# The second mixer's second gate as four seven-product pairs, with the forms made beside the first gate

## The chip, the core and the metric

The kernel runs on one core of one Trainium2 chip. The metric is device time in microseconds (us) for one execution, the median of several; the profile is of one execution.

## The reference

Two transformer blocks are applied to 512 tokens of 1024 features in float32: a first mixer, an MLP with a gated side input, a second mixer and a second MLP. The change lies in the second mixer. There a normed input is projected, two branches are computed (`ya`, a windowed attention, and `yb`, a gated linear attention), each goes through a matrix of its own, and two gates weigh them:

```
h = rmsnorm(x, ln_mix_g[l]);  z = h @ w_in[l];  qa, ..., ga, gb = split_cols(z)
merged = sigmoid(ga) * (ya @ w_branch_a[l]) + sigmoid(gb) * (yb @ w_branch_b[l])
x = x + merged @ w_out[l]
```

Every matrix here has 1024 columns, that is 8 output tiles of 128; `h`, `yb` and `merged` are 1024 wide (8 input blocks of 128), `ya` is 512 wide (4 blocks).

## The kernel before

Activations lie feature by feature: 128 partitions x 8 blocks x 512 tokens. A *tile* is one output of 128 features x 512 tokens in a bank of PSUM. It is summed over its blocks, and each block takes three matmuls of 512 columns (L1728 to L1730), because both operands are split in a high and a low part (`AH`/`AL` for the normed input, `WH`/`WL` for weights): high x high, low x high, high x low.

Weights stream in *chunks* of eight blocks (512 KB). SyncE loads a chunk into one of three raw buffers (`w_load`, L1645), ScalarE copies it to the high part (`w_hi`, L2156), VectorE makes the low part (`w_lo`, L2561). Four converted units are held (`NW`); a conversion waits until the unit four before it has been used. `ahead` says the conversion of three units ahead when TensorE begins a chunk, and `rest` says the low part and the load from the fifth block on.

A *pair* (`pair`) computes two output tiles of one normed input by seven products instead of eight, over halves of the tokens (256 columns) and halves of the input blocks. Each product is 12 matmuls of 256 columns (L1709 to L1711). The order of products is

```
SLOTS = (1, 5, 6, 2, 7, 3, 4)
```

and a pair needs four converted units from its two chunks: sums of weights (`s_add` 1 and 2, kept in `WS`), the first chunk (with high and low part whole), half a chunk (`s_add` 4, whose copy is L2154) and the second chunk (after `s_add` 3). `s_snap` has ScalarE copy a finished product from PSUM (`SN`) so that the bank can go on summing: product 6 waits for the snapshot of product 1, product 4 for that of product 7. VectorE then adds what is missing (`s_c11`, `s_c12`, `s_c22`). The input side of products 5, 6, 7 and 4 are four *forms* of the normed input: `t_diff` (GpSimd, L3363), `t_u` (ScalarE), `t_2`, `t_3`, `t_4` (VectorE), and then `t_split` 1 to 4, in which ScalarE makes the high part (L2182 for form 1 in four pieces, L2186) and VectorE the low part (L2635, L2640). Form 4 is written over a part of `AH`/`AL`, so it waits for the last plain tile. Before the change pairs serve the first MLP (stage "2") and the second (stage "5"); each stage has buffers of its own, a fourth raw buffer (`WX`) among them.

One order is written out by hand, step by step (`say`), and each engine's program takes its steps from it in that order; an engine waits for semaphores where a step needs another engine's. `beside` runs a list of steps alongside the blocks (one `tick` per block, two per product of a pair), `finish` says what is left of them at once, `align` fills the running chunk with empty blocks.

At the end of the second mixer (`mixer2`) the order of TensorE is: first gate tiles 0 and 1, then tile m of branch a and gate tile m+2 in turn, two tiles of the second gate, then tile m of branch b and second-gate tile m+2 in turn (all plain tiles of eight blocks, those of branch a of four), and the output projection (`mix2`). For a gate tile VectorE multiplies by the norm's factor (`scaled`, L2971) and ScalarE takes the sigmoid (L2482, L2487). Branch b is multiplied by its gate (L3222), added to branch a's (L3226), and split for the output projection (L2491, L2655). Six empty blocks stand ahead of the second MLP's first down blocks, where `align` is called; the gates begin two blocks into a chunk.

Of the kernel before, what the change touches and what calls it, by code (L numbers as in the profile page):

```python
# [196 lines left out]
class Order:  # L197


    def __init__(self, sections=()):  # L200
        self.found = []
        self.cut = set()
        self.npairs = 0
        self.pair_of = {}
        self.last_plain = {}
        self.in_stage = {}
        self.last_pair = {}
        self.units = []
# [184 lines left out]
    def forms(self, s, n=5):  # L393

        self.say("t_diff", s)
        yield 4
        self.say("t_u", s)
        yield 3
        self.say("t_2", s)
        yield 3  # L400
        self.say("t_3", s)
        yield 3
        self.say("t_4", s)
        yield 3
        for j in range(1, n):
            self.say("t_split", s, j)
            yield 3
# [604 lines left out]
    def mixer2(self, post):  # L1012
# [57 lines left out]
        def gate_a(m):  # L1070
            t = self.tile(fm(at("ga", 128 * m)), A)
            self.say("gate_a", m, t)
            self.close(t)
        gate_a(0)
# [273 lines left out]
class Memory:  # L1348
    def __init__(self, nc, dram, psum):
# [96 lines left out]
        self.MGL = at("MGL", 90, [128, 8, T], F32R)  # L1446
        self.GA = at("GA", 78, [128, 2, T])
        self.GB = at("GB", 66, [128, 4, T])
# [14 lines left out]
        self.AC4 = at("AC4", 110.25, [128, T])  # L1463
# [31 lines left out]
    def x(self, kind, j):  # L1495

        h, l = {"A": (self.AH, self.AL), "B1": (self.BH, self.BL), "D1": (self.DH, self.DL), "C1": (self.CHh, self.CLl),
                "F1": (self.FH1, self.FL1), "P1": (self.PH, self.PL), "Y2": (self.YAH, self.YAL),
                "Z2": (self.YBH, self.YBL), "M2": (self.MGH, self.MGL), "F2": (self.FH2, self.FL2)}[
                    "A" if kind[0] == "A" else kind]  # L1500
        if kind in ("F1", "F2"):
            j = j % (FS if kind == "F1" else FS2)
        return h[:, j, :], l[:, j, :]

    def raw(self, b):

        return self.WR[:, b, :] if b < NRAW else (self.WX1, self.WX2)[b - NRAW][:]

    def t_raw(self, s, j):

        if j < 4:
            return (self.TW1 if s == "2" else self.TW2)[:, j - 1, :, :]
        return self.sn(s)[:, :, :]

    def t_form(self, s, j):

        if j < 4:
            h, l = (self.TH1, self.TL1) if s == "2" else (self.TH2, self.TL2)
            return h[:, j - 1, :, :], l[:, j - 1, :, :]
        return tuple(a[:, :, :].rearrange("p (i q) t -> p i q t", q=2)[:, :, 0, T // 2:] for a in (self.AH, self.AL))  # L1520
# [9 lines left out]
    def sn(self, s):  # L1530
        return self.SN1 if s == "2" else self.SN2
# [6 lines left out]
    def ws(self, s):  # L1538
        return self.WS1 if s == "2" else self.WS2
# [77 lines left out]
def sync_program(e, w, order, at, m):  # L1617
# [17 lines left out]
    def w_load(c):  # L1635
# [7 lines left out]
        elif b >= NRAW:  # L1643
            w.wait_ge(*at("rbc", "25"[b - NRAW]))
# [28 lines left out]
def tensor_program(e, w, order, at, m):  # L1673
# [262 lines left out]
    def values1(u, t):  # L1936
# [12 lines left out]
        ins.then_inc(*at.up("values1", "values1", u))  # L1949
# [86 lines left out]
    def values2(u, t):  # L2036
# [12 lines left out]
        ins.then_inc(*at.up("values2", "values2", u))  # L2049
# [93 lines left out]
def scalar_program(e, w, order, at, m):  # L2143
# [25 lines left out]
    def t_u(s):  # L2169
        w.wait_ge(*at("rbc", s))  # L2170
        for i in range(4):
# [5 lines left out]
    def t_split(s, j):  # L2177
        h, x = m.t_form(s, j)[0], m.t_raw(s, j)
        w.wait_ge(*at(("t_diff", "t_2", "t_3", "t_4")[j - 1], s))
        if j == 1:  # L2180
# [56 lines left out]
    def exp1(u):  # L2237
# [3 lines left out]
        if u >= 2:  # L2241
            w.wait_ge(*at("turn1", u - 2))
        e.activation(m.PB1[:, u % 2, 0:W], m.SB1[:, u % 2, 0:W], ACT.Exp, scale=-1.0, bias=col[:, 0:1],
                     accum_out=col[:, 1:2]).then_inc(*at.up("exp1", "exp1", u))

    def scale1(u):
        p = m.PB1[:, u % 2, 0:128 * (unit1(u)[1] + 1)]
        w.wait_ge(*at("recip1", u))
        e.activation(p, p, ACT.Copy, scale=m.ST1[:, 6 + 3 * u:7 + 3 * u]).then_inc(*at.up("probs1", "probs1", u))

    def turned1(u, t):
# [5 lines left out]
        e.activation(m.PT1[:, u % 2, 0:W], m.bank[t.bank][:, 0:W], ACT.Copy).then_inc(*at.up("turned1", "turned1", u))  # L2257
# [124 lines left out]
    def exp2(u):  # L2382
# [3 lines left out]
        for g in range(2):  # L2386
            s = m.SB2[:, u % 2, W * g:W * g + W]
            e.activation(s, s, ACT.Exp, scale=-1.0, bias=col(g), accum_out=col(6 + g)).then_inc(*at.up("exp2", "exp2", u, g))
        w.wait_ge(*at("sink2", u))
        e.activation(col(4, 2), col(2, 2), ACT.Exp).then_inc(*at.up("exp2", "exp2", u))  # L2390

    def scale2(u):
        W = 256 if u % 4 else 128
        w.wait_ge(*at("recip2", u))
        for g in range(2):
            s = m.SB2[:, u % 2, W * g:W * g + W]
            e.activation(s, s, ACT.Copy, scale=m.WST[:, 10 * u + 8 + g:10 * u + 9 + g]).then_inc(
                *at.up("probs2", "probs2", u))

    def turn2(u, t):  # L2400
# [5 lines left out]
        e.activation(m.PT2[:, u % 2, 0:W], m.bank[t.bank][:, 0:W], ACT.Copy).then_inc(*at.up("turned2", "turned2", u))  # L2406
# [77 lines left out]
    def gate_b(i, t):  # L2484
        g = m.GB[:, i % 4, :]
        w.wait_ge(*at("gate_b", i))
        e.activation(g, g, ACT.Sigmoid).then_inc(*at.up("gate_sig", "gb_sig", i))  # L2487

    def branch_b(i, t):
# [35 lines left out]
    def ffn_u(f, t):  # L2525
        if f < 6:
# [10 lines left out]
           "gn_out": gn_out, "vb": vb, "rb_silu": rb_silu, "ya_split": ya_split, "gate_a": gate_a, "gate_b": gate_b,  # L2537
           "branch_b": branch_b, "ffn_a": ffn_a, "ffn_u": ffn_u}
# [5 lines left out]
def vector_program(e, w, order, at, m):  # L2544
# [18 lines left out]
    def s_add(c, j):  # L2563
# [4 lines left out]
        if j == 1:  # L2568
            w.wait_ge(*at("w_raw", c + 1))
            w.wait_ge(*at("rbc", s))  # L2570
            if order.units_before(c) is not None:
                w.wait_ge(*at("w_lo", order.units_before(c)))
# [32 lines left out]
    def t_2(s):  # L2605
        w.wait_ge(*at("t_diff", s))
# [154 lines left out]
    def scale1(u):  # L2761
        col = m.ST1[:, 4 + 3 * u:7 + 3 * u]
        w.wait_ge(*at("exp1", u))
        e.reciprocal(col[:, 2:3], col[:, 1:2]).then_inc(*at.up("recip1", "recip1", u))
# [304 lines left out]
    def scale2(u):  # L3069
        col = lambda i, k=1: m.WST[:, 10 * u + i:10 * u + i + k]  # L3070
        w.wait_ge(*at("exp2", u))
        for g in range(2):
            e.tensor_scalar(col(6 + g), col(6 + g), col(4 + g), None, ALU.add).then_inc(*at.up("recip2", "total2", u))
        w.wait_ge(*at("total2", u))
        e.reciprocal(col(8, 2), col(6, 2)).then_inc(*at.up("recip2", "recip2", u))
# [134 lines left out]
    def gate_b(i, t):  # L3210
        if i >= 4:
            w.wait_ge(*at("x_lo", "M2", i - 4))
        else:
            w.wait_ge(*at("yb", 7))
        scaled(m.GB[:, i % 4, :], t, "4").then_inc(*at.up("gate_b", "gate_b", i))
        at.also(("gate_b", i), "read", t.id)

    def branch_b(i, t):
# [8 lines left out]
        low("M2", i, g)  # L3227
# [84 lines left out]
    def y_base(i):  # L3312
# [17 lines left out]
           "gate_a": gate_a, "branch_a": branch_a, "gate_b": gate_b, "branch_b": branch_b, "mix2": mix2, "ffn_a": ffn_a,  # L3330
# [6 lines left out]
def gpsimd_program(e, w, order, at, m):  # L3337
# [19 lines left out]
    def t_diff(s):  # L3357
        for i in range(0, 8, 2):
            for b in range(2):
                w.wait_ge(*at("h", s, i, b))  # L3360
        x = m.H[:, :, :].rearrange("p (i q) t -> p i q t", q=2)[:, :, 0, :]
# [309 lines left out]
```

## Time and profile before

| what | value |
|---|---|
| three runs | 1427.6, 1427.9, 1428.74 us; median 1427.9 |
| the profiled execution's own time | 1427.68 us |
| its span, first to last instruction | 1425.9 us |
| busy | PE 1413.9, DVE 986.4, ACT 647.0, POOL 214.8 us |
| granted TensorE clock, mean | 0.998 |

PE is TensorE's matmuls, PEld its weight loads, DVE VectorE, ACT ScalarE, POOL GpSimd, SP SyncE. Starts are us from the span's start. A matmul's end in the trace is modelled, and the next starts before it; the spacing of starts tells what one costs.

### The profile page before, as it was taken

The page shows a single profiled execution, that of the slowest core. Times are in us where ns is not written, and L with a number is a line of the kernel's source. Part 1 is how long each engine was busy: PE and PEld are TensorE (multiplying, and loading weights), DVE is VectorE, ACT ScalarE, POOL GpSimd, SP SyncE. Part 2 cuts the span into 40 slices and gives each one's busy share as a digit, 9 for nine tenths or more (in the row PEclk, how much of TensorE's full clock was granted, in tenths as well). Part 3 has the DMA queues.
Part 4 walks back from the last instruction along what each step waited for, and adds up shares of the span by engine and source line. Part 5 has one row for each costly group of instructions (what it writes and reads, how often), then busy time and mean ns, then how long its engine had stood idle before and what let it go on. Part 6 is the DMA issues. An engine that isn't in the chain of part 4 may idle for free.

```text
span 1425.9 us, 20562 instructions
## 1 busy us (share of the span) xinstructions
PE 1413.9 (99%) x8054; PEld 1213.9 (85%) x8054; DVE 986.4 (69%) x1537; ACT 647.0 (45%) x1028; POOL 214.8 (15%) x136
## 2 busy tenths in 40 slices
PE   9999999999999999999999999999999999999998
PEld 6776798889989888887799888888888889999997
DVE  5777477876676657897696736534452888888877
ACT  5345535534345434545464546323332545455450
POOL 4175224000000011330052104000021000000000
PEclk9999999999999999999999999999999999999999
DMA  6222212333233332222211211323323233333331
GB/s 242 89 75 69 65 60 89 100 97 115 93 100 104 119 104 74 89 67 82 74 60 41 65 45 59 110 90 101 98 90 92 87 105 103 103 93 116 104 106 73
DMA packets 36352, 130.00 MB, mean 91 GB/s; under 512 B 4040, under 2 KB 4296, under 8 KB 36256
## 3 DMA queue, kind: packets, MB, share of 16 engines
q1 hardware_dynamic: 35968, 128.44, 28.5%
q8 instruction: 64, 1.05, 0.3%
q14 instruction: 32, 0.26, 0.1%
q10 hardware_dynamic: 288, 0.26, 0.1%
HBM read 126.56 MB, written 2.10 MB: 90 GB/s over the span
## 4 chain that ended last, share of the span: by engine, by line
PE 91%; DVE 5%; ACT 2%; issue 1%; DMA 1%; ACTq 0%; DVEq 0%; SPq 0%
PE P L1728 17%; PE P L1730 16%; PE P L1729 16%; PE P L1709 5%; PE P L1711 5%; PE P L1710 5%; PE P L1776 4%; PE P L1767 4%; PE P L1769 4%; PE P L2069 2%; DVE WL L2561 1%; PE P L1816 1%; PE P L1817 1%; PE P L1818 1%; PE P L1924 1%
## 5 line engine op out<-in xcount | busy, mean ns | idle before, releaser
L2156 ACT ACTIVATE WH<-WR 128x1024 fp32r<-128x1024 f32 x212 | 223.6, 1055 | 259.2 <-PE P L1730 181.4
L2561 DVE TENSOR_TENSOR WL<-WR,WH 128x1024 fp32r<-128x1024 f32 x196 | 265.5, 1355 | 103.0 <-ACT WH L2156 102.6
L1728 PE MATMUL P<-AH,WH 128*128 128x512 f32 x456 | 186.2, 408 | 0.2 <-DVE BC L3002 0.2
L1730 PE MATMUL P<-AH,WL 128*128 128x512 f32 x456 | 178.2, 391 | 0.0
L1729 PE MATMUL P<-AL,WH 128*128 128x512 f32 x456 | 177.8, 390 | 0.0
L1728 PE MATMUL P<-FH,WH 128*128 128x512 f32 x432 | 168.5, 390 | 0.5 <-issue 0.3
L1729 PE MATMUL P<-FL,WH 128*128 128x512 f32 x432 | 168.4, 390 | 0.0
L1730 PE MATMUL P<-FH,WL 128*128 128x512 f32 x432 | 168.1, 389 | 0.0
L3375 POOL TENSOR_TENSOR AC<-AC,SQ 128x512 f32<-128x512 f32 x27 | 42.5, 1573 | 506.7 <-ACT SQ L2211 505.8
L1709 PE MATMUL P<-AH,WH 128*128 128x256 f32 x400 | 113.5, 284 | 0.3 <-ACT SN L2167 0.2
L1711 PE MATMUL P<-AH,WL 128*128 128x256 f32 x400 | 113.2, 283 | 0.0
L1710 PE MATMUL P<-AL,WH 128*128 128x256 f32 x400 | 113.2, 283 | 0.0
L1728 PEld LDWEIGHTS P<-AH,WH 128*128 128x128 f32 x456 | 85.7, 188 | 21.1 <-issue 4.5
L1730 PEld LDWEIGHTS P<-AH,WL 128*128 128x128 f32 x456 | 85.6, 188 | 18.6
L1729 PEld LDWEIGHTS P<-AL,WH 128*128 128x128 f32 x456 | 85.9, 188 | 16.3 <-issue 0.5
L1767 PE MATMUL P<-AH,WH 128*128 128x512 f32 (+1 forms) x264 | 96.0, 371 | 1.9 <-ACT AH L2202 1.6
L1728 PEld LDWEIGHTS P<-FH,WH 128*128 128x128 f32 x432 | 81.2, 188 | 17.5 <-issue 0.7
L1769 PE MATMUL P<-AH,WL 128*128 128x512 f32 (+1 forms) x264 | 95.2, 367 | 0.8 <-DVE WL L2561 0.5
L1730 PEld LDWEIGHTS P<-FH,WL 128*128 128x128 f32 x432 | 81.1, 188 | 17.1
L1729 PEld LDWEIGHTS P<-FL,WH 128*128 128x128 f32 x432 | 81.2, 188 | 15.8
L1709 PE MATMUL P<-TH,WH 128*128 128x256 f32 x300 | 84.9, 283 | 0.0
L1710 PE MATMUL P<-TL,WH 128*128 128x256 f32 x300 | 84.9, 283 | 0.0
(409 smaller groups left out, 3148.0 us busy)
## 6 DMA issues: line engine op xcount, KB each, us to landing
WR<-in_ws SPq DMA_DIRECT2D x212, 512.0 KB, 3.5
WX<-in_ws SPq DMA_DIRECT2D x21, 512.0 KB, 3.5
out<-Y SPq DMA_DIRECT2D x8, 256.0 KB, 2.0
H<-in_xT SPq DMA_DIRECT2D x3, 512.0 KB, 8.0
C<-in_const SPq DMA_DIRECT2D x1, 946.5 KB, 11.0
H<-in_xT SPq DMA_DIRECT2D x2, 256.0 KB, 4.4
PR<-in_pT SPq DMA_DIRECT2D x1, 512.0 KB, 4.9
WR<-in_ws SPq DMA_DIRECT2D x1, 384.0 KB, 4.8
```

Of the source, the lines that this page charges most:

```text
L1709: e.matmul(P, wh, xh, start=k in (1, 5, 2) and i == 0, stop=False, skip_group_check=True)
L1710: e.matmul(P, wh, xl, start=False, stop=False, skip_group_check=True)
L1711: ins = e.matmul(P, wl, xh, start=False, stop=k in (2, 3, 4) and i == 3, skip_group_check=True)
L1728: e.matmul(P, wh, xh, start=start, stop=False)
L1729: e.matmul(P, wh, xl, start=False, stop=False)
L1730: ins = e.matmul(P, wl, xh, start=False, stop=stop)
L1767: e.matmul(P, m.WH[:, c % NW, o:o + 128], xh, start=start, stop=False, skip_group_check=True)
L1769: e.matmul(P, m.WL[:, c % NW, o:o + 128], xh, start=False, stop=False, skip_group_check=True)
L1776: ins = e.matmul(m.bank[t.bank][:, cols(a)], wh, m.x(*x)[1][:, cols(a)], start=False, stop=stop, skip_group_check=True)
L2156: e.activation(H, w_source(m, order, k), ACT.Copy).then_inc(*at.up("w_hi", "w_hi", k))
L2561: e.tensor_tensor(L, w_source(m, order, k), H, ALU.subtract).then_inc(*at.up("w_lo", "w_lo", k))
L3375: e.tensor_tensor(AC, AC, m.square(n, i)[:, cols(a)], ALU.add).then_inc(*at.up("summed", "summed", n, i, parts(a)[0]))
```

## The change

The second gate's eight tiles become four pairs (stage "4"), each followed by two tiles of branch b. The forms are made beside the first gate: the raw ones from the fifth tile of branch a on, the splits after the last tile of the first gate. `align` is called ahead of the first pair, and six banks serve the ring during the pairs. The split of a merged tile becomes a step of its own (`merged_split`), said one block after an even tile, and inside the next pair after an odd one. Stage "4" gets buffers of its own (a fourth raw buffer `WX3`, loaded once `yb` is done), others move to make room, and some semaphores of steps that never run together are merged. The total number of blocks stays 1872. Steps for a first gate in pairs (`kind` "a", `gated_a`, `branch_a_copy`) are written but not called.

```diff
-        for s, buffer in (("2", NRAW), ("5", NRAW + 1)):
+        for s, buffer in (("2", NRAW), ("5", NRAW + 1), ("4", NRAW + 2)):
...
             t = self.tile(specs, [("Y2", j) for j in range(4)])
-            self.finish((lambda: self.yb == 8) if m < 4 else (lambda: self.gated))
+            if m < 5:
+                self.finish((lambda: self.yb == 8) if m < 4 else None)
+            if m == 4:
+                self.beside(self.raws("4", 3))
             self.say("branch_a", m, t)
             self.close(t)
             if m < 6:
-                gate_a(m + 2)
-
-        def gate(m):
-            t = self.tile(fm(at("gb", 128 * m)), A)
-            self.say("gate_b", m, t)
-            self.close(t)
-        gate(0)
-        gate(1)
+                t = gate_a(m + 2)
+            if m == 5:
+                self.last_plain["4"] = t
+                self.beside(self.splits("4", range(1, 5), 3))
         self.finish()
-        for m in range(8):
+        self.banks = (0, 1, 2, 3, 6, 7)
+        self.align()
+
+        def post(p):
+            kind, i = p.f
+            self.say("gate_first", p, kind, i)
+            self.say("gate_sig", kind, i)
+            yield 1
+            self.say("gate_second", p, kind, i + 1)
+            self.close(p.x)
+            self.say("gate_sig", kind, i + 1)
+            yield 2
...
+        def pair(kind, i):
+            c0 = at("g" + kind, 128 * i)
+            self.pair("4", fm(c0), fm(c0 + 128), (kind, i), post)
+
+        def branch(m):
             t = self.tile([block("w_branch_b_2", 128 * q, 128 * m) for q in range(8)], [("Z2", q) for q in range(8)])
             self.say("branch_b", m, t)
             self.close(t)
-            if m < 6:
-                gate(m + 2)
+            self.beside(merged(m))
+
+        def merged(m):
+            yield 10 if m % 2 and m < 7 else 1
+            self.say("merged_split", m)
+        for m in range(0, 8, 2):
+            pair("b", m)
+            branch(m)
+            branch(m + 1)
+        self.finish()
+        self.banks = (0, 1, 2, 3)
...
+    def gate_first(p, kind, i):
+        gate_free(kind, i)
+        w.wait_ge(*at("s_c11", p.id))
+        w.wait_ge(*at("s_c12", p.id))
+        e.tensor_tensor(m.gate(kind, i), m.snap(p, 0, 2), m.RBC3[:], ALU.mult).then_inc(
+            *at.up("gate_" + kind, "gate_" + kind, i))
+
+    def gate_second(p, kind, i):
+        g = m.gate(kind, i)
+        gate_free(kind, i)
+        w.wait_ge(*at("s_full", p.id, 4))
+        e.tensor_tensor(g[:, cols(0)], m.bank[p.x.bank][:, cols(0)], m.RBC3[:, cols(0)], ALU.mult).then_inc(
+            *at.up("gate_" + kind, "gate_half", kind, i))
+        at.also(("gate_half", kind, i), "read", p.x.id)
+        w.wait_ge(*at("s_c22", p.id))
+        e.tensor_tensor(g[:, cols(1)], m.snap(p, 3), m.RBC3[:, cols(1)], ALU.mult).then_inc(
+            *at.up("gate_" + kind, "gate_" + kind, i))
+        at.also(("gate_" + kind, i), "sn_free", p.id)
...
+    def merged_split(i):
+        low("M2", i, m.GB[:, i % 4, :])
```

## Rows read from the trace of the kernel before

**Rows 1.** The page: busy time, share, instructions by engine; the chain that ended last.

```profile
PE 1413.9 (99%) x8054; PEld 1213.9 (85%) x8054; DVE 986.4 (69%) x1537; ACT 647.0 (45%) x1028; POOL 214.8 (15%) x136
...
PE 91%; DVE 5%; ACT 2%; issue 1%; DMA 1%; ACTq 0%; DVEq 0%; SPq 0%
```

**Rows 2.** Timeline of TensorE, second gate and branch b: start, duration, line, operation.

```profile
939.81 0.39 PE L1728 MATMUL P<-AH,WH 128*128 128x512 f32 x1
...
1026.85 0.39 PE L1728 MATMUL P<-MGH,WH 128*128 128x512 f32 x1
```

**Rows 3.** Timeline of TensorE, a pair of the first MLP.

```profile
299.37 0.28 PE L1709 MATMUL P<-AH,WH 128*128 128x256 f32 x1
...
309.44 0.40 PE L1728 MATMUL P<-FH,WH 128*128 128x512 f32 x1
```

**Rows 4.** Windows: a pair's period in the first MLP; the gate stage.

```profile
core 0: us, PE busy (x) PEld busy (x) DVE busy (x) ACT busy (x) POOL busy (x), PEclk, DMA share, GB/s
...
299.37:320.35 20.98, 20.98 (x134) 19.09 (x133) 14.52 (x20) 8.88 (x13) 0.00 (x0) 1.00 0.32 101
...
945.00:1031.00 86.00, 86.00 (x381) 71.20 (x380) 40.30 (x48) 26.25 (x32) 0.00 (x0) 1.00 0.30 92
```

**Rows 5.** Timeline of TensorE and VectorE, last MLP, around its first pairs.

```profile
1158.83 0.39 PE L1728 MATMUL P<-FH,WH 128*128 128x512 f32 x1
...
1163.45 1.22 DVE L2561 TENSOR_TENSOR WL<-WR,WH 128x1024 fp32r<-128x1024 f32 x1
...
1164.77 0.47 PE L1728 MATMUL P<-FH,WH 128*128 128x512 f32 x1 [0.33 <-issue]
...
1170.31 0.28 PE L1709 MATMUL P<-AH,WH 128*128 128x256 f32 x1
...
1180.71 0.40 PE L1728 MATMUL P<-FH,WH 128*128 128x512 f32 x1
...
1210.96 0.39 PE L1709 MATMUL P<-AH,WH 128*128 128x256 f32 x1 [0.19 <-ACT SN L2167]
```

**Rows 6.** Tiles of forms and snapshots: duration ns min/median/max, first and last start.

```profile
L2167 ACT ACTIVATE SN<-P x100: 360/384/388, 280.5 to 1381.0; 128x256 f32<-128x256 f32 x100
...
L2182 ACT ACTIVATE TH<-TW,PM x8: 493/495/498, 266.1 to 1145.0; 128x256 fp32r<-128x256 f32 x8
L2635 DVE SCALAR_TENSOR_TENSOR TL<-TW,PM,TH x8: 477/480/485, 267.9 to 1146.8; 128x256 fp32r<-128x256 f32 x8
L2186 ACT ACTIVATE TH<-TW x4: 1042/1044/1045, 267.7 to 1147.3; 128x1024 fp32r<-128x1024 f32 x4
L2640 DVE TENSOR_TENSOR TL<-TW,TH x4: 1219/1221/1226, 269.5 to 1149.4; 128x1024 fp32r<-128x1024 f32 x4
L3363 POOL TENSOR_TENSOR TW<-H x2: 2404/2786/3167, 229.0 to 1076.0; 128x1024 f32<-128x1024 f32 x2
```

**Rows 7.** Timeline of ScalarE and VectorE at the last tile of the first gate.

```profile
934.64 0.69 DVE L2971 TENSOR_TENSOR GA<-P,RBC 128x512 f32<-128x512 f32 x1 [3.69 <-PE P L1730]
...
935.25 1.22 DVE L2561 TENSOR_TENSOR WL<-WR,WH 128x1024 fp32r<-128x1024 f32 x1
...
935.37 0.63 ACT L2482 ACTIVATE GA<-GA 128x512 f32<-128x512 f32 x1 [1.03 <-DVE GA L2971]
```

**Rows 8.** Timeline of VectorE and TensorE at the first pair of the first MLP.

```profile
276.94 1.22 DVE L2561 TENSOR_TENSOR WL<-WX,WH 128x1024 fp32r<-128x1024 f32 x1
...
277.88 0.39 PE L1730 MATMUL P<-FH,WL 128*128 128x512 f32 x1
278.31 0.36 PE L1709 MATMUL P<-AH,WH 128*128 128x256 f32 x1
```

**Rows 9.** Timeline of VectorE and ScalarE, last MLP: fourth weight sum, half copy.

```profile
1182.87 0.69 DVE L2581 TENSOR_TENSOR WR<-WR,WS 128x512 f32<-128x512 f32 x1
...
1183.59 0.63 ACT L2154 ACTIVATE WH<-WR 128x512 fp32r<-128x512 f32 x1 [3.33 <-DVE WR L2581]
```

More of the change, by code:

```diff
@@ L393, in forms, with raws, splits @@
     def forms(self, s, n=5):
+        yield from self.raws(s, 3)
+        yield from self.splits(s, range(1, n), 3)
+    def raws(self, s, pace):
         self.say("t_diff", s)
-        yield 4
+        yield pace + 1
         self.say("t_u", s)
-        yield 3
+        yield pace
         self.say("t_2", s)
-        yield 3
+        yield pace
         self.say("t_3", s)
-        yield 3
+        yield pace
         self.say("t_4", s)
-        yield 3
-        for j in range(1, n):
+        yield pace
+    def splits(self, s, js, pace):
+        for j in js:
             self.say("t_split", s, j)
-            yield 3
+            yield pace
     def narrow(self, name, c0, n, kind):
@@ L1073, in gate_a @@
             self.close(t)
+            return t
         gate_a(0)
@@ L1498, in x @@
                 "F1": (self.FH1, self.FL1), "P1": (self.PH, self.PL), "Y2": (self.YAH, self.YAL),
-                "Z2": (self.YBH, self.YBL), "M2": (self.MGH, self.MGL), "F2": (self.FH2, self.FL2)}[
+                "Z2": (self.YBH, self.YBL), "M2": (self.MGH, (self.MGLA, self.MGLB)[j // 4 % 2]), "F2": (self.FH2, self.FL2)}[
                     "A" if kind[0] == "A" else kind]
+        if kind == "M2":
+            return h[:, j, :], l[:, j % 4, :]
         if kind in ("F1", "F2"):
@@ L1505, in raw @@
     def raw(self, b):
-        return self.WR[:, b, :] if b < NRAW else (self.WX1, self.WX2)[b - NRAW][:]
+        return self.WR[:, b, :] if b < NRAW else (self.WX1, self.WX2, self.WX3)[b - NRAW][:]
     def t_raw(self, s, j):
         if j < 4:
+            if s == "4":
+                return self.TW3A[:, 0, :, :] if j == 1 else self.TW3B[:, j - 2, :, :]
             return (self.TW1 if s == "2" else self.TW2)[:, j - 1, :, :]
@@ L1517, in t_form @@
         if j < 4:
+            if s == "4":
+                l = self.TL3A[:, 0, :, :] if j == 1 else self.TL3B[:, j - 2, :, :]
+                return self.TH3[:, j - 1, :, :], l
             h, l = (self.TH1, self.TL1) if s == "2" else (self.TH2, self.TL2)
@@ L1530, in sn, with gate @@
     def sn(self, s):
-        return self.SN1 if s == "2" else self.SN2
+        return {"2": self.SN1, "4": self.SN3, "5": self.SN2}[s]
+    def gate(self, kind, i):
+        return self.GA[:, i % 2, :] if kind == "a" else self.GB[:, i % 4, :]
     def snap(self, p, j, n=1):
@@ L1538, in ws @@
     def ws(self, s):
-        return self.WS1 if s == "2" else self.WS2
+        return {"2": self.WS1, "4": self.WS3, "5": self.WS2}[s]
     def sq(self, n):
@@ L2179, in t_split @@
         w.wait_ge(*at(("t_diff", "t_2", "t_3", "t_4")[j - 1], s))
+        if s == "4" and j < 4:
+            w.wait_ge(*at("x_lo", "Z2", 2 * j - 1))
         if j == 1:
@@ L2256, in turned1 @@
             w.wait_ge(*at("values1", u - 2))
-        e.activation(m.PT1[:, u % 2, 0:W], m.bank[t.bank][:, 0:W], ACT.Copy).then_inc(*at.up("turned1", "turned1", u))
+        e.activation(m.PT1[:, u % 2, 0:W], m.bank[t.bank][:, 0:W], ACT.Copy).then_inc(*at.up("turned", "turned1", u))
         at.also(("turned1", u), "read", t.id)
@@ L2405, in turn2 @@
             w.wait_ge(*at("values2", u - 2))
-        e.activation(m.PT2[:, u % 2, 0:W], m.bank[t.bank][:, 0:W], ACT.Copy).then_inc(*at.up("turned2", "turned2", u))
+        e.activation(m.PT2[:, u % 2, 0:W], m.bank[t.bank][:, 0:W], ACT.Copy).then_inc(*at.up("turned", "turned2", u))
         at.also(("turned2", u), "read", t.id)
@@ L2482, in gate_a, with gate_sig, branch_a_copy @@
         e.activation(g, g, ACT.Sigmoid).then_inc(*at.up("gate_sig", "ga_sig", i))
[L2484 to L2489, printed above, removed]
+    def gate_sig(kind, i):
+        g = m.gate(kind, i)
+        w.wait_ge(*at("gate_" + kind, i))
+        e.activation(g, g, ACT.Sigmoid).then_inc(*at.up("gate_sig", "g%s_sig" % kind, i))
+    def branch_a_copy(i, t):
+        w.wait_ge(*at("full", t.id))
+        w.wait_ge(*at("yb", 7))
+        if i >= 4:
+            w.wait_ge(*at("gn_gated", 7))
+        e.activation(m.MG[:, i, :], m.bank[t.bank][:], ACT.Copy).then_inc(
+            *at.up("branch_a_copy", "branch_a_copy", i))
+        at.also(("branch_a_copy", i), "read", t.id)
+    def merged_split(i):
         w.wait_ge(*at("merged", i))
@@ L3208, in branch_a, with gated_a, gate_free @@
         at.also(("branch_a", i), "read", t.id)
-    def gate_b(i, t):
-        if i >= 4:
-            w.wait_ge(*at("x_lo", "M2", i - 4))
-        else:
-            w.wait_ge(*at("yb", 7))
-        scaled(m.GB[:, i % 4, :], t, "4").then_inc(*at.up("gate_b", "gate_b", i))
-        at.also(("gate_b", i), "read", t.id)
+    def gated_a(i):
+        x = m.MG[:, i, :]
+        w.wait_ge(*at("branch_a_copy", i))
+        w.wait_ge(*at("ga_sig", i))
+        e.tensor_tensor(x, x, m.GA[:, i % 2, :], ALU.mult).then_inc(*at.up("branch_a", "branch_a", i))
+    def gate_free(kind, i):
+        if kind == "a":
+            w.wait_ge(*at("branch_a", i - 2))
+        else:
+            w.wait_ge(*(at("x_lo", "M2", i - 4) if i >= 4 else at("gn_gated", 7)))
+    def gate_first(p, kind, i):
[5 more added lines that the diff above has]
+    def gate_second(p, kind, i):
+        g = m.gate(kind, i)
+        gate_free(kind, i)
[7 more added lines that the diff above has]
+        at.also(("gate_" + kind, i), "sn_free", p.id)
     def branch_b(i, t):
@@ L3226, in branch_b, with merged_split @@
         e.tensor_tensor(g, g, m.MG[:, i, :], ALU.add).then_inc(*at.up("branch_b", "merged", i))
-        low("M2", i, g)
+    def merged_split(i):
+        low("M2", i, m.GB[:, i % 4, :])
     def mix2(i, t):
```

55 lines of the change are left out of this document (38 added, 17 removed).

## The prediction, made before the result was known

> **What bounds the kernel now.** I read the page first. TensorE is busy for 99% of the span and fills 91% of the chain that ended last [rows 1]. So a part of this change counts only if it makes TensorE's queue shorter or makes TensorE wait. Next I read the timeline of TensorE over the stage. The first matmul of the second gate starts at 939.81 and the first of the output projection at 1026.85 [rows 2]. Between them lie 16 plain tiles of 24 matmuls: 87.04 us, 5.44 us a tile, 0.2267 us a matmul of 512 columns, without a hole. Third, the timeline of the first MLP, which has pairs already: a pair starts at 299.37 and the plain blocks behind it at 309.44 [rows 3]; the next pair follows 20.98 us after the first [rows 4]. So the 84 matmuls of a pair take 10.07 us (0.12 us each), where the two plain tiles that they replace take 10.88. Fourth, the windows: over one such period of 20.98 us VectorE is busy for 14.52 and ScalarE for 8.88, in the present gate stage for 40.30 and 26.25 of 86 [rows 4]. Neither is the bound on average, so the rest is a matter of order.
>
> **The change, part by part.** *Removed:* eight plain gate tiles, 8 x 5.44 = 43.52 us of TensorE, with eight VectorE multiplies of 512 columns. *Added on TensorE:* four pairs, 4 x 10.07 = 40.28. The eight tiles of the second branch stay. In steady state the stage costs four periods of pair and 16 blocks, which is the period in rows 4: 4 x 20.98 = 83.92 against 87.04, **-3.1 us**. That is 7%, not the 12.5% of saved columns, because a matmul of half the columns costs 0.53 of a full one.
>
> The Trainium skill, "TensorE: Matmul & The Clock Gate", section "Back-to-back issue gap", gives 262 cycles for 256 columns and 518 for 512; an estimate by these would be 9.2 against 10.4 us, so about 4.8 us for four pairs. The row has 10.07 against 10.88, and the sum goes by the row.
>
> *Added on the other engines per pair:* four sums of weights (0.69 each), four weight splits (three of 1.22 us on VectorE, one of 0.69) in place of two of 1.22, four snapshots on ScalarE (0.38 each [rows 6]), three half-width combinations, and the two gates. From the 14.52 us of VectorE in rows 4 I take off the first MLP's own work in that period (two relu squares, two splits, three accumulations: 4.8 us) and add the gates (0.69 + 2 x 0.42), and multiply, add and split for two branch tiles (6 x 0.69): 15.4 of 20.98. That hides behind the pair. Without this cover each added VectorE microsecond would cost one. The weight transfers are the same in number, and a fourth raw buffer is added for this stage; the first MLP has the same four chunks a period and no hole, so I cost them at nothing.
>
> *The forms:* one GpSimd subtraction (2.4 to 3.2 us [rows 6]); on ScalarE four small scalings and then the splits (four of 0.495 and three of 1.04, 5.1 us); on VectorE twelve small operations and the low parts (four of 0.48 and three of 1.22). The first half, up to the raw forms, is queued behind the fifth tile of branch a, some 19 us before the first pair. VectorE has idle stretches there, so it costs nothing. The splits are queued only behind the last gate tile, and that is eight blocks (5.44 us) before the pair. Here I follow the queues of both engines, since each takes its steps in the written order. The times are those of the timeline of before, in which the pair's first product would be due at 939.81.
>
> - VectorE multiplies the last gate tile at 934.64, the sigmoid follows at 935.37 and ends at 936.0 [rows 7]. Only then comes form 1 on ScalarE: four pieces, 1.7 us as a row of four, to 937.6. VectorE, which used to split weights at 935.25 [rows 7], is now queued behind form 1 and idles until 937.7; its four pieces end at 939.3.
> - Behind them stands the low part of the pair's first weight chunk: 1.22 us, to 940.5. TensorE needs it for the first product. In the first MLP such a split began at 276.94 and the pair at 278.31 [rows 8], so 0.15 us pass from its end to TensorE. The pair starts at 940.65, **0.84 us late**.
> - Behind that split VectorE makes the fourth weight sum (0.69, to 941.3). ScalarE's half copy must wait for it, as in the last MLP, where the sum starts at 1182.87 and the copy at 1183.59 [rows 9]. Forms 3 and 4 are queued behind this copy, then the full copy of the second chunk, and only then the snapshot of the first product. That is 0.63 + 2 x 1.04 + 1.06 + 0.38, less about 0.1 of overlap at each step: the snapshot ends near 945.1. The third product adds into the same bank and waits for it. It was due two products (2 x 1.44) after the start, at 943.6, so **1.65 us more**.
> - VectorE meanwhile has form 2, two branch products, forms 3 and 4 and two weight splits, near 947.6. The fifth product needs the last of these at 948.1: just hidden.
>
> The first pair therefore costs **+2.5 us**. From below this is bounded by nothing at all (if the queues drained as in the first MLP, whose first pair began 0.43 us after the matmul before it, 0.2 late [rows 8]); from above by about 3.2, if these operations run 10% slower side by side and the fifth product waits too. I take the worked chain.
>
> *Moved:* the alignment. The gate's pairs must start on a chunk, so six empty blocks are put in here, and the six that stood ahead of the last MLP's first down blocks go. There TensorE now loses time: a chunk takes from 1158.83 to 1164.77, 0.50 more than 5.44 and 0.07 behind it, and a weight split of VectorE ends just before, at 1163.45 + 1.22; the pair after it takes 10.40 instead of 10.07 [rows 5]. With a whole chunk ahead, that split comes 4 us earlier. I take the 0.57 back, **-0.6**; the bounds are 0 and -0.9. The buffer moves and the merged semaphores add no instruction, and the output projection keeps its order: its last operand is split while its first seven blocks run, as before.
>
> **The sum.** -3.1 + 2.5 - 0.6 = -1.2 us, against the profiled execution's own 1427.68 (span 1425.9, 1.78 around it): 1426.5. The median of the three runs lies 0.2 above that execution, so I predict 1426.7. A difference under 0.2%, 2.9 us, can't be told from no change here.
>
> **The rivals.**
> - *The cover suffices.* The splits drain as in the first MLP and the first pair loses 0.3 instead of 2.5: 1424.5 with the 0.2 of the median. For it: every steady pair there runs without a hole [rows 3]. Against: there the forms had 32 more blocks of cover; here they have eight. Chance 0.15.
> - *Half the columns, half the time.* If 256 columns took half of 0.2267, a pair would take 9.52, 5.4 us saved in four: 1424.4. The Trainium skill's page named above leans that way. Against: the row of 10.07. Chance 0.03.
> - *Every later pair waits too: slower.* The split of the merged odd tile stands on ScalarE ahead of the snapshot of the fifth product, which the seventh and last waits for. A pair of the last MLP already waits there (1210.96 [rows 5]). The fifth product ends 7.2 us into its pair; with that split (0.63) and its own 0.38 the snapshot ends near 7.95, and the last product is due at 8.64, 0.7 later. If it comes more than 0.7 us late, three pairs pay the excess; at 2.1 us late each pays 1.4 and the time is 1430.9. Against: VectorE is less loaded here than in the last MLP, and the period is that of the first. Chance 0.06.
> - *More comes back in the last MLP, or the stall is smaller by a microsecond.* 1425.4. Chance 0.14.
> - *My forecast*, 1425.9 to 1428.0 with its own bounds (stall 2.0 to 3.2, return 0 to 0.9): chance 0.62.
>
> **The numbers.** Faster by over 0.2% is below 1425.0: the first two rivals nearly whole and a few hundredths of the fourth, 0.19. Slower is above 1430.8: about half of the third and what I have not thought of, 0.05. The rest, 0.76, is no change. The range of 8 in 10 reaches into the first rival on one side and to the end of the forecast with 0.8 more on the other: 1424.5 to 1428.8.
>
> **What the profile after would show.** If I am right: steady pairs of 10.07 us and periods of 20.98 in the stage; in the first pair a hole of 0.8 us before its first matmul, released by VectorE's weight split, and one of 1.6 before its third product, released by ScalarE's snapshot; in ScalarE's queue an idle stretch of near 2.8 us before the half copy, with forms 3 and 4 behind it; the output projection starting near 1026.2 instead of 1026.85; the hole at 1164.77 gone. I am wrong if the stage runs without holes and ends near 1024, if later pairs have holes, or if the hole of the last MLP stays or a new one opens where its chunks have shifted.

## The result, and the profile after

The changed kernel takes 1431.94 us (median of 9 runs, 1430.72 to 1432.76) where the kernel before took 1427.6 beside it: a ratio of 1.0029, 95% interval 1.0020 to 1.0038. It is slower by 4.3 us, outside my range. The profiled span is 1430.1 us, 4.2 above before.

Page after: busy time by engine, and the chain that ended last.

```profile
PE 1415.0 (99%) x8198; PEld 1221.2 (85%) x8198; DVE 1012.5 (71%) x1596; ACT 664.3 (46%) x1063; POOL 216.2 (15%) x137
...
PE 85%; DVE 8%; ACT 4%; issue 1%; DMA 1%; SPq 0%; DVEq 0%; ACTq 0%
```

Beside [rows 1]: TensorE's share of the chain fell from 91% to 85%, VectorE's and ScalarE's rose from 5 and 2 to 8 and 4. TensorE's "busy" didn't fall by the 3.1 us that the pairs save, it rose by 1.1. Waits have come in, and something has made matmuls longer.

Timeline of TensorE after, the stage (rows answering to [rows 2] and [rows 3]):

```profile
940.39 0.39 PE L1785 MATMUL P<-YAH,WL 128*128 128x512 f32 x1
941.39 0.36 PE L1764 MATMUL P<-AH,WH 128*128 128x256 f32 x1 [0.62 <-DVE WL L2629]
...
944.22 0.28 PE L1766 MATMUL P<-TH,WL 128*128 128x256 f32 x1
947.18 0.39 PE L1764 MATMUL P<-TH,WH 128*128 128x256 f32 x1 [2.68 <-ACT SN L2222]
...
955.96 0.40 PE L1783 MATMUL P<-YBH,WH 128*128 128x512 f32 x1
...
966.87 0.28 PE L1764 MATMUL P<-AH,WH 128*128 128x256 f32 x1
...
1029.81 0.39 PE L1783 MATMUL P<-MGH,WH 128*128 128x512 f32 x1
```

Read the gaps between starts. The first pair was due at 940.39 + 0.23 = 940.62 and its plain tiles begin at 955.96: 15.34 us instead of 10.07, where I had 12.6. It loses 0.85 ahead of the first product, 2.94 ahead of the third, and about 1.5 more behind that. From 966.87 on nothing is lost: the other three periods end at 1029.81, 3 x 20.98 later.

Windows of TensorE after (stretch; length, busy and count; granted clock; DMA share; GB/s):

```profile
941.40:947.10 5.70, 3.10 (x24) 1.00 0.00 0
947.20:951.20 4.00, 4.00 (x21) 0.57 0.62 210
951.20:955.90 4.70, 4.70 (x41) 1.00 0.46 156
```

Here is the third loss. After the idle stretch the granted clock is 0.57 in the mean of 4 us: about 15 matmuls of 256 columns stand 0.21 us apart instead of 0.12, the 1.2 GHz level of the clock instead of 2.4.

Timeline of VectorE and ScalarE after, the queue ahead of the third product, in order of time:

```profile
934.08 1.06 ACT L2211 ACTIVATE WH<-WX 128x1024 fp32r<-128x1024 f32 x1 [4.23 <-PE P L1785]
...
935.45 0.69 DVE L3043 TENSOR_TENSOR GA<-P,RBC 128x512 f32<-128x512 f32 x1 [2.10 <-PE P L1785]
...
936.71 1.69 ACT L2241 ACTIVATE TH<-TW3A,PM 128x256 fp32r<-128x256 f32 x4
...
938.43 1.68 DVE L2707 SCALAR_TENSOR_TENSOR TL3A<-TW3A,PM,TH 128x256 fp32r<-128x256 f32 x4 [2.30 <-ACT TH L2241]
...
940.03 1.22 DVE L2629 TENSOR_TENSOR WL<-WX,WH 128x1024 fp32r<-128x1024 f32 x1
...
942.08 0.64 ACT L2209 ACTIVATE WH<-WX 128x512 fp32r<-128x512 f32 x1 [2.72 <-DVE WX L2651]
...
944.51 1.04 ACT L2211 ACTIVATE WH<-WR 128x1024 fp32r<-128x1024 f32 x1
...
945.43 1.21 DVE L2712 TENSOR_TENSOR AL<-SN,AH 128x1024 fp32r<-128x1024 f32 x1
...
946.74 0.66 ACT L2222 ACTIVATE SN<-P 128x256 f32<-128x256 f32 x2 [1.19 <-DVE AL L2712]
```

Up to 945.5 this is the chain that I had worked out, 0.8 later because this execution reached the stage 0.8 later: from 188 to 194 us, where the code is the same, its granted clock is 0.72, in the execution of before 1.00. (The change doesn't bring this: *before2* below, with the code of before up there, has 0.72 as well.) But then ScalarE, done with its weight copy, idles 1.19 us more before the snapshot, and the releaser is VectorE's low part of form 4 (`AL`). The raw form 4 lies in the snapshot buffer `SN`, so a stage's first snapshot must wait until it is split: `s_snap` has a wait for `t_lo(s, 4)` when no pair precedes. I had queued the snapshot behind ScalarE's work alone.

Timeline of VectorE, TensorE, ScalarE and SyncE's queue after, last MLP (answering to [rows 5]):

```profile
1168.68 1.22 DVE L2629 TENSOR_TENSOR WL<-WS,WH 128x1024 fp32r<-128x1024 f32 x1
1169.81 0.68 DVE L3380 TENSOR_TENSOR GG<-P,SS 128x512 f32<-128x512 f32 x1
...
1170.55 0.50 PE L1783 MATMUL P<-FH,WH 128*128 128x512 f32 x1 [0.38 <-DVE GG L3380]
...
1173.76 0.36 PE L1764 MATMUL P<-AH,WH 128*128 128x256 f32 x1 [0.20 <-DVE WL L2629]
...
1176.66 0.68 DVE L2626 TENSOR_TENSOR WL<-WX,WH 128x512 fp32r<-128x512 f32 x1
...
1177.42 0.33 SPq L1700 DMA_DIRECT2D WX<-in_ws  x1
...
1180.83 0.69 DVE L2651 TENSOR_TENSOR WS<-WX 128x512 f32<-128x512 f32 x1 [1.75 <-DMA WX<-in_ws]
...
1182.35 1.06 ACT L2211 ACTIVATE WH<-WS 128x1024 fp32r<-128x1024 f32 x1 [2.62 <-DVE WS L2651]
1183.32 0.37 ACT L2222 ACTIVATE SN<-P 128x256 f32<-128x256 f32 x1
...
1183.74 0.39 PE L1764 MATMUL P<-AH,WH 128*128 128x256 f32 x1 [1.05 <-ACT SN L2222]
```

The hole of before is gone from its place. There the first matmul of a chunk, at 1164.77, came 0.10 us after the end of that chunk's low part (1163.45 + 1.22 [rows 5]); now this low part is made from 1164.52 to 1165.74, and its chunk starts at 1167.29 without a hole. But one tile later 0.65 us are lost at 1170.55, then 0.43 at the first pair's start, and 1.31 ahead of its seventh product at 1183.74. From the bottom up, the last of these: that product waits for a snapshot, the snapshot stands on ScalarE behind a weight copy, that waits for VectorE's sum, the sum for a transfer, and the transfer was issued (1177.42) when VectorE had made the half chunk's low part (1176.66). That is 2.9 us after the pair's start; in the kernel before it was 1.8, against the 1170.31 of [rows 5]:

```profile
1172.12 0.68 DVE L2558 TENSOR_TENSOR WL<-WX,WH 128x512 fp32r<-128x512 f32 x1
```

Ahead of all this a weight split (1168.68) now stands before `GG`, VectorE's product of a hidden tile, which reads a bank of PSUM and so frees it; TensorE's next tile waits for that (1170.55).

So the span's 4.2 us are: steady stage -3.12, first pair +5.27, last MLP +1.25, and 0.81 from this execution.

### The profile page after: what moved, and what is told of

The parts are those of the page before. It is cut to its first block, busy times and chain, and to the rows that moved or that the text cites. A ratio compares the mean times of both kernels' runs of the same rounds, so it can differ in the third digit from the quotient of the medians.

```text
span 1430.1 us, 20946 instructions
## 1 busy us (share of the span) xinstructions
PE 1415.0 (99%) x8198; PEld 1221.2 (85%) x8198; DVE 1012.5 (71%) x1596; ACT 664.3 (46%) x1063; POOL 216.2 (15%) x137
## 4 chain that ended last, share of the span: by engine, by line
PE 85%; DVE 8%; ACT 4%; issue 1%; DMA 1%; SPq 0%; DVEq 0%; ACTq 0%
PE P L1783 14%; PE P L1785 14%; PE P L1784 14%; PE P L1764 6%; PE P L1765 6%; PE P L1766 6%; PE P L1831 4%; PE P L1822 4%; PE P L1824 4%; DVE WL L2629 2%; PE P L2124 1%; PE P L1871 1%; ACT WH L2211 1%; PE P L1872 1%; PE P L1873 1%
## 5 line engine op out<-in xcount | busy, mean ns | idle before, releaser
L2629 DVE TENSOR_TENSOR WL<-WR,WH 128x1024 fp32r<-128x1024 f32 x192 | 254.8, 1328 | 116.3 <-ACT WH L2211 116.1
L1783 PE MATMUL P<-AH,WH 128*128 128x512 f32 x392 | 161.4, 412 | 0.1
L1785 PE MATMUL P<-AH,WL 128*128 128x512 f32 x392 | 153.3, 391 | 0.0
L1784 PE MATMUL P<-AL,WH 128*128 128x512 f32 x392 | 152.9, 390 | 0.0
L1764 PE MATMUL P<-AH,WH 128*128 128x256 f32 x464 | 132.1, 285 | 2.0 <-ACT SN L2222 1.0
L1765 PE MATMUL P<-AL,WH 128*128 128x256 f32 x464 | 131.7, 284 | 0.0
L1766 PE MATMUL P<-AH,WL 128*128 128x256 f32 x464 | 131.6, 284 | 0.0
L1764 PE MATMUL P<-TH,WH 128*128 128x256 f32 x348 | 99.0, 285 | 2.7 <-ACT SN L2222 2.7
L1766 PE MATMUL P<-TH,WL 128*128 128x256 f32 x348 | 98.9, 284 | 0.0
L1764 PEld LDWEIGHTS P<-AH,WH 128*128 128x128 f32 x464 | 89.3, 193 | 4.7 <-issue 2.0
L1783 PEld LDWEIGHTS P<-AH,WH 128*128 128x128 f32 x392 | 73.7, 188 | 18.7 <-issue 4.5
```

The source lines that it names most:

```text
L1764: e.matmul(P, wh, xh, start=k in (1, 5, 2) and i == 0, stop=False, skip_group_check=True)
L1765: e.matmul(P, wh, xl, start=False, stop=False, skip_group_check=True)
L1766: ins = e.matmul(P, wl, xh, start=False, stop=k in (2, 3, 4) and i == 3, skip_group_check=True)
L1783: e.matmul(P, wh, xh, start=start, stop=False)
L1784: e.matmul(P, wh, xl, start=False, stop=False)
L1785: ins = e.matmul(P, wl, xh, start=False, stop=stop)
```

## The experiments

Each kernel was timed beside the kernel before on the same chip. The ratios, with their 95% intervals, are the measure; 0.001 is 1.4 us.

| kernel | median us | ratio | interval | first pair | loss in last MLP |
|---|---|---|---|---|---|
| changed | 1431.94 | 1.0029 | 1.0020 to 1.0038 | 15.3 | 3.1 |
| early | 1426.16 | 0.9993 | 0.9984 to 1.0002 | 10.1 | 3.2 |
| phase | 1429.99 | 1.0021 | 1.0012 to 1.0029 | 15.4 | 1.9 |
| moved | 1429.05 | 1.0009 | 1.0000 to 1.0017 | none | 2.6 |
| both | 1424.83 | 0.9983 | 0.9975 to 0.9992 | 10.1 | 1.4 |
| own | 1429.17 | 1.0012 | 1.0004 to 1.0021 | 12.6 | 3.5 |
| fill | 1430.97 | 1.0023 | 1.0014 to 1.0032 | 13.9 | 3.2 |
| hole | 1431.26 | 1.0022 | 1.0013 to 1.0031 | 14.3 | 3.7 |
| shift4 | 1422.75 | 0.9970 | 0.9960 to 0.9981 | 10.1 | 0 |
| shift6 | 1431.34 | 1.0031 | 1.0020 to 1.0043 | 10.1 | 8.0 |
| before2 | 1426.82 | 0.9989 | 0.9981 to 0.9998 | none | 0 |
| after4 | 1429.17 | 1.0010 | 1.0001 to 1.0019 | 15.4 | 0 |

The last two columns are us from the trace: from the due start of the first gate pair to the plain tile behind it, and the sum of all spacings in excess of 0.2267 and 0.12 us in the tail of the last MLP's plain tiles and in its pairs. The kernel before has 1.8 in the last column.

**early.** The splits of forms 1 to 3 right behind the raw forms, form 4 beside the next branch tile.

```diff
             if m == 4:
-                self.beside(self.raws("4", 3))
+                self.beside(chain([self.raws("4", 3), self.splits("4", (1, 2, 3), 1)]))
...
             if m == 5:
                 self.last_plain["4"] = t
-                self.beside(self.splits("4", range(1, 5), 3))
+                self.beside(fourth())
```

`chain` runs its lists one after the other; `fourth` says `t_split` 4 after three blocks.

> The changed kernel with forms 1 to 3 split right behind the last raw form (beside the last first-gate tile) instead of behind its sigmoid, and form 4 split a few blocks later, beside the branch tile that follows; nothing else differs. Theory A (the first pair waits because the splits start at 936.7 us, so that the weights' low part and the first snapshot come late, and the long idle stretch then costs clock): the first pair takes 10.1 to 10.9 us from the end of the plain tile ahead of it instead of 15.3, its matmuls stay 0.12 us apart, and the span falls by 4.4 to 5.3 us against the changed kernel: about 1427. Rival B (the splits only move the queue of VectorE and ScalarE onto something else, the weights' low parts or the last gate's sigmoid): the idle time stays at 2 to 4 us in all around the first pair, and the time is 1429 to 1431. Neither touches the last MLP.

Timeline of ScalarE, VectorE and TensorE of this kernel:

```profile
928.73 1.69 ACT L2248 ACTIVATE TH<-TW3A,PM 128x256 fp32r<-128x256 f32 x4
...
936.84 1.22 DVE L2636 TENSOR_TENSOR WL<-WX,WH 128x1024 fp32r<-128x1024 f32 x1
...
938.77 1.22 DVE L2719 TENSOR_TENSOR AL<-SN,AH 128x1024 fp32r<-128x1024 f32 x1
...
939.60 0.28 PE L1771 MATMUL P<-AH,WH 128*128 128x256 f32 x1
...
949.67 0.40 PE L1790 MATMUL P<-YBH,WH 128*128 128x512 f32 x1
```

Counted from the pair's due start, form 1 begins 7 us earlier (10.9 us ahead of it instead of 3.9), where the rows of the changed kernel show ScalarE idle for 4.23 us and then VectorE for 2.10; the first chunk's low part ends at 938.1 and form 4's at 940.0. The pair takes 10.07 us, without a hole. The ratio falls by 0.0036, 5.1 us: theory A, not B. All of the first pair's loss comes from where the splits stand in the queues.

**own.** The raw form 4 in 4 KB apart from the snapshots, a place that is free once `yb` is split (one more wait in `t_4`, left out here); the splits stay late.

```diff
-        return self.sn(s)[:, :, :]
+        return (self.SR3 if s == "4" else self.sn(s))[:, :, :]
...
-                w.wait_ge(*at("t_lo", p.s, 4))
+                w.wait_ge(*at("t_4" if p.s == "4" else "t_lo", p.s, *(() if p.s == "4" else (4,))))
```

> The changed kernel with form 4's raw values in a buffer of their own, so that the first pair's first snapshot waits for the raw form alone and no longer for VectorE's low part of form 4; the splits stay as late as they are. Theory A (the overlooked wait is one of several late steps): the snapshot then stands only behind ScalarE's copy of the next weight part, which ends at 945.5 us, so the hole before the third product shrinks from 2.84 to about 1.65 us as my prediction had it; but the weights' low part of the fourth product ends at 948.4 us as before, so about 1.0 us comes back as a hole ahead of the fourth product, and the pair ends 0.4 to 1.8 us earlier, by how much of the half-speed stretch is left: 1430.1 to 1431.5. Rival E (the overlooked wait alone made my sum wrong): the first pair falls to my predicted 12.6 us, 2.7 us less: 1429.2.

Timeline of TensorE of this kernel:

```profile
941.91 0.36 PE L1765 MATMUL P<-AH,WH 128*128 128x256 f32 x1 [0.62 <-DVE WL L2630]
...
946.38 0.39 PE L1765 MATMUL P<-TH,WH 128*128 128x256 f32 x1 [1.37 <-ACT SN L2223]
...
953.68 0.40 PE L1784 MATMUL P<-YBH,WH 128*128 128x512 f32 x1
```

Due at 941.13, ended at 953.68: 12.55 us, 2.8 less than in the changed kernel, and the holes are 0.85 and 1.62 where my prediction had 0.84 and 1.65. The clock stays at 1.00. So E is right for the first pair, and my expectation under A was wrong: it gave the second chunk's low part to the fourth product. That low part runs from 947.68 to 948.90, and the fourth product starts without a hole at 947.92; only the fifth needs it, as the prediction had said. The one overlooked wait cost 1.3 us of hole, and the longer hole then cost the clock.

**fill.** The changed kernel with eleven unused products into an unused bank ahead of the third product.

```diff
+        if k == 6 and p.s == "4" and p.before is None:
+            w.wait_ge(*at("x_lo", "Z2", 7))
+            for i in range(11):
+                e.matmul(m.bank[4][:], m.WH[:, u % NW, 512 * half:512 * half + 128], m.YBH[:, i % 8, :],
+                         start=True, stop=True)
```

> The changed kernel with eleven 512-column products into an unused bank between the first pair's second and third products, so that TensorE works on while it waits; their result is used by nobody and the wait itself is left as it is. Theory F (the 15 products at 0.21 us come from the idle stretch ahead of them): the third product starts as late as before, within 0.2 us, its products come 0.12 us apart, and the span falls by 1.3 to 1.5 us: 1430.5. Rival G (the slow products belong to the products' own late operands or to the pairs): they stay 0.21 us apart and the time is 1431.9, or more by what the eleven products overrun.

Windows of this kernel, the filled stretch and the one behind it:

```profile
944.50:947.30 2.80, 2.73 (x13) 1.00 0.00 0
947.40:951.20 3.80, 3.80 (x32) 1.00 0.65 195
```

The third product starts as late as before, but the granted clock stays at 1.00 and the pair takes 13.9 instead of 15.3 us. The ratio falls by 0.0006 (0.9 us), which the intervals don't separate from none; the trace does. Theory F.

**hole.** The early splits, and four copies of 128 x 800 that nobody needs ahead of the first snapshot.

```diff
                 w.wait_ge(*at("t_lo", p.s, 4))
+                if p.s == "4":
+                    w.wait_ge(*at("x_lo", "Z2", 7))
+                    for i in range(4):
+                        if i:
+                            w.wait_ge(*at("idle", i - 1))
+                        e.activation(m.SR3[:, :, 0:400], m.H[:, 0:2, 0:400], ACT.Copy).then_inc(
+                            *at.up("gate_sig", "idle", i))
```

> The kernel with the early splits, with four copies of 128 x 800 on ScalarE ahead of the first pair's first snapshot, which nobody needs: the operands are all there, and the third product waits for the snapshot alone, about 2.5 to 3 us. Theory F (an idle stretch of that length costs clock besides its own length): slow products of 0.21 us follow, and the time is that of the early splits, 1426.2, and 3.5 to 4.4 us: 1429.7 to 1430.6. Rival G: the hole costs its own length and no more, 1428.7 to 1429.2, and the products behind it are 0.12 us apart.

Windows of this kernel, the hole, and a stretch that begins 1.6 us behind it:

```profile
943.20:945.80 2.60, 0.20 (x2) 1.00 0.74 236
...
947.50:951.00 3.50, 3.50 (x19) 0.52 0.01 2
```

The pair takes 14.3 us, 4.2 more than in *early*; the hole is 2.76 of these, the slow matmuls the rest. In the ratios it is 0.0029, 4.1 us. Theory F again: with operands all there, that hole costs half as much again.

**phase** and **moved.** Two empty blocks ahead of the output projection of the changed kernel (`self.weight(())` twice, one more chunk), and in the kernel before an `align` at that place.

> The changed kernel with two empty blocks ahead of the second mixer's output projection, so that every weight chunk from there on starts at the same block as in the kernel before (one more chunk is loaded, and the padding of six comes ahead of the last MLP's pairs again). Theory C (the last MLP lost its 1.3 us because the shifted chunks bring the weights' conversion into other places of the queues): its idle places go back to those of the kernel before (0.57 us before the second plain product, 0.2 to 0.45 at the first pairs), and the span falls by 1.2 to 1.9 us: about 1430.4. Rival D (it lost them from something that the stage leaves behind, or from the execution alone): no change, 1431.9. The first pair of the gate stays at 15.3 us by both.

> The kernel before, with one alignment to a chunk (six empty blocks) ahead of the output projection, which takes the place of the one ahead of the last MLP's pairs: the last MLP then has the chunk positions of the changed kernel, and nothing else of the change is there. Theory C (positions of chunks): the last MLP shows the idle places of the changed kernel (about 0.5 us ahead of a plain tile at its tail, 1.2 us in the second pair), and the time is 1.3 to 1.9 us above before: 1428.9 to 1429.5. Rival D (something else): the same as before, 1427.6, with the old idle places. My prediction's step for this part was a gain: 1427.0.

Timeline of TensorE, the first pair's seventh product: phase, then moved.

```profile
1181.59 0.39 PE L1766 MATMUL P<-AH,WH 128*128 128x256 f32 x1 [0.21 <-ACT SN L2224]
```

```profile
1180.01 0.39 PE L1710 MATMUL P<-AH,WH 128*128 128x256 f32 x1 [0.99 <-ACT SN L2168]
```

With the old chunk positions the changed kernel's hole shrinks from 1.31 to 0.47 us; with the new ones the kernel before, which has nothing else of the change, gets it, 1.25 us. The last MLP loses 1.2 us less and 0.8 more, and the ratios move by -0.0008 and +0.0009. Each alone is near what its interval can tell, but traces and signs agree: theory C. **both** joins *early* and *phase*.

> Early splits and the old chunk positions together. Theories A and C: the two parts add, 4.4 to 5.3 and 1.2 to 1.9 us, from 1431.9: 1424.7 to 1426.3, faster than the kernel before by 0.1 to 0.2%. With B and D: 1429 to 1431. With A and D: 1427. With B and C: 1428 to 1430.

It came out at 1424.83, at the lower end of the sum of A and C.

**shift4** and **shift6** are *early* with four and six empty blocks at that place.

> The early splits with four empty blocks ahead of the output projection in place of two (or none): another position of the chunks in the last MLP, nothing else. Theory C (the position decides which conversions stand between the work of the last plain tiles): the idle places of the last MLP's tail and first pairs differ from both earlier positions, the rest of the trace is that of the early splits; the time lies within 1.5 us of the two positions measured, 1424.8 and 1426.2. Rival H (only the old position is good, the rest are like the shifted one): 1426.2, with about 1.3 us at the seventh product of the first pair.

> The early splits with six empty blocks ahead of the output projection. By theory C a fourth pattern of idle places in the last MLP, time within 1.5 us of 1424.8 to 1426.2; by rival H 1426.2 with about 1.3 us at the seventh product of the first pair.

Both left the band that I had given, one on each side. Timeline of VectorE around the same product `GG`, that of the last plain tile: shift4, then shift6, there with TensorE's next tile.

```profile
1158.48 0.69 DVE L3389 TENSOR_TENSOR GG<-P,SS 128x512 f32<-128x512 f32 x1 [0.76 <-PE P L1794]
1159.38 1.23 DVE L2638 TENSOR_TENSOR WL<-WS,WH 128x1024 fp32r<-128x1024 f32 x1 [0.20 <-ACT WH L2220]
```

```profile
1167.48 1.23 DVE L2638 TENSOR_TENSOR WL<-WS,WH 128x1024 fp32r<-128x1024 f32 x1 [1.65 <-ACT WH L2220]
1168.63 0.68 DVE L3389 TENSOR_TENSOR GG<-P,SS 128x512 f32<-128x512 f32 x1
...
1169.37 0.50 PE L1792 MATMUL P<-FH,WH 128*128 128x512 f32 x1 [1.53 <-DVE GG L3389]
```

In shift4 `GG` waits only for its own matmuls and the weight split comes behind it. In shift6 the split is queued ahead of `GG` and itself waits for ScalarE, so TensorE, which needs the bank that `GG` reads, loses 1.8 us. It loses more one chunk earlier. Timeline of VectorE in shift4, then of ScalarE, VectorE and TensorE in shift6 for the same chunk, with shift6's window behind it:

```profile
1150.72 1.23 DVE L2638 TENSOR_TENSOR WL<-WR,WH 128x1024 fp32r<-128x1024 f32 x1 [0.20 <-ACT WH L2220]
```

```profile
1154.85 0.63 ACT L2583 ACTIVATE SS<-SS 128x512 f32<-128x512 f32 x1 [1.61 <-DVE SS L3380]
1155.39 1.04 ACT L2220 ACTIVATE WH<-WR 128x1024 fp32r<-128x1024 f32 x1
...
1156.46 1.23 DVE L2638 TENSOR_TENSOR WL<-WR,WH 128x1024 fp32r<-128x1024 f32 x1 [1.65 <-ACT WH L2220]
...
1157.79 0.47 PE L1792 MATMUL P<-FH,WH 128*128 128x512 f32 x1 [1.99 <-issue]
```

```profile
1158.70:1161.90 3.20, 3.20 (x9) 0.52 0.47 169
```

The matmul at 1157.79 is the first of a chunk. The profile names no releaser for it, but that chunk's low part ends 0.10 us before it, and stands behind ScalarE's copy, which is queued behind a hidden tile's activation (`SS`). In shift4 the same low part starts at 1150.72, the chunk at 1155.53, without a hole. So shift6 has a hole of 2.2 us, then matmuls of 512 columns 0.43 us apart at a granted clock of 0.52. Theory C holds. Rival H does not, by shift4, whose last MLP has no hole at all (in shift6 the seventh product of the first pair loses 1.4 us as well). But positions are worth far more than I gave them: 8.6 us between the best and the worst of the four tried.

**before2** (two empty blocks in the kernel before) and **after4** (four in the changed one) put both at the position of shift4.

> The kernel before with two empty blocks ahead of the output projection, so that its last MLP has the chunk position at which the early splits showed no idle place there; the second gate stays plain. Theory C: the last MLP's idle places of the kernel before (0.57, 0.33, 0.28, 0.45 and 0.19 us, 1.8 in all) go, and the time falls by about 1.8 us: 1425.2 to 1425.8. Against the early splits at this position (1422.75) it then stands 3.1 us higher by the pairs alone, the term of my sum. Rival (the early splits at this position gain by something that the pairs bring): no fall, 1427.0.

> The changed kernel as it was made, with four empty blocks ahead of the output projection: the same position in the last MLP as the other kernel of this call, and the first pair with its late splits. Theories A and C: its last MLP has no idle place, its first pair takes 15.3 us, so it stands 5.3 us above the early splits at this position, at 1428.0, and 2 to 2.5 us (steady gain 3.1, first pair 5.2) above the kernel before at this position. Rival: 1430 or more, if the last MLP's loss belongs to the delay of the first pair.

At this position no last MLP has a hole, so what is left is the stage alone: shift4 stands 0.0019 below before2 (2.7 us; the steady term is 3.1), after4 stands 0.0021 above it (3.0; expected 2 to 2.5) and 0.0040 above shift4 (5.7; the first pair's 5.3). shift4 is the fastest kernel here, 0.30% below the kernel before; 0.11% of this is the position, which the kernel before could have had.

## Why the prediction was wrong, point by point

- *Steady stage, -3.1:* right. shift4 runs the whole stage from 939.63 to 1023.55, 83.92 us to the hundredth. Half the columns in half the time (9.52 a pair) is ruled out again: pairs take 10.07.
- *First product 0.84 late:* right, 0.85.
- *The sum* is 5.5 us below the profiled execution (1426.5 against 1432.01): 1.3 for a wait that it doesn't have, 1.5 for a lower clock behind the longer hole, 1.9 for the last MLP, 0.8 for this execution.
- *Third product 1.65 late:* **the step that failed first.** It has the snapshot wait for ScalarE's queue alone. It also waits for VectorE's low part of form 4, because raw form 4 and snapshots share a buffer: 2.94. With that wait gone (*own*) the step's own number stands, 1.62.
- *What a hole costs:* the prediction counted a hole at its length. The holes of 0.85 and 1.62 us in *own* did cost that. Behind those of 2.94 in the changed kernel, 2.76 in *hole* and 2.2 in shift6 came matmuls at the lower clock, which cost 1.5 to 1.6 us more each time; the prediction has no term for this. *fill* keeps the wait, fills it, and is rid of this part. The Trainium skill, "TensorE: Matmul & The Clock Gate", section "Back-to-back issue gap", gives the spacing at the lower clock as columns over 1.2, in ns; an estimate by it is 213 ns for 256 columns and 427 for 512. The rows agree with it: 0.21 and 0.43 us.
- *Last MLP, -0.6:* **failed too**, wrong in sign. I saw that the split of weights ends just before the hole and moved it 4 us earlier by the position of the chunk. That hole did go (the split now ends 1.55 us ahead of its chunk), but I had not followed VectorE's queue in the new order behind it. There another split stands ahead of `GG`, and the half chunk comes 1.1 us later to its load. It is +1.3, of which *phase* gives 1.2 back and *moved* makes 0.8.
- *The rivals:* none came. Later pairs had no holes, so the merged tile's split on ScalarE is covered. That the cover suffices was false for the order as made, but true of the place 7 us earlier, which I had counted as idle time of VectorE and not compared with the splits.

What stays open: the stage is reached between 939.5 and 941.1 in different executions of the same code. The five with a granted clock of 0.72 from 188 to 194 us (the changed kernel, *both*, *own*, *fill*, *before2*) reach it from 940.6 on, the eight with 1.00 by 940.4; why the clock differs there is not shown. Nor are the last 0.2 to 0.5 us between ratios and traces explained.

## What to carry to other kernels

When work is moved in front of a stage, follow every wait of the first use on every engine, buffers that are shared included, and look for the earliest idle stretch that can take it, not the last place that is still legal. Look behind a hole of TensorE as well as at it: the matmuls that follow may run at the lower clock, and that belongs to its price. And when an edit shifts where chunks begin, compare positions at once: two empty blocks can be worth more than the edit, and a change is only judged fairly when both kernels stand at the same position, or each at the best one tried.

## What the runs showed of the hardware

- A single wait of TensorE in an otherwise full stretch was followed by the 1.2 GHz level in five kernels: 2.94 us in the changed kernel, *phase* and *after4* (each 0.57 over the 4 us behind it), 2.76 in *hole* (0.52) and 2.2 in *shift6* (0.52). In *hole* the operands were all there. Behind the waits of 0.85 and 1.62 us in *own* the clock stayed at 1.00.
- The fall came up to 1.5 us after matmuls had begun again (in *hole* they restart at 945.91 with 0.12 us between them and slow down from 947.44 on), so the loss is not seen at the hole itself.
